# The chunked form of a bidirectional state-space scan, inside a two-block transformer kernel

## The chip, the cores and the metric

The program runs on one core of a Trainium2 chip. Its time is device microseconds for one launch, from inputs in HBM to the output in HBM; smaller is better. Before the change it takes 3826.4 us (median of three runs, 3825.4 to 3835.86).

## What is computed

The kernel computes a whole model step for 512 tokens of width 1024: a first block (a feed-forward layer, a mixer, a second feed-forward layer, with a context of 256 tokens beside it) and a second block of two layers. The change touches the mixer of the first block alone. Cut to what matters, with 12 heads in 4 groups, head width 64, state width 128:

```python
CHUNK = 128
def ssd_chunked(xs, dt, a, bm, cm, h0):          # one direction
    xdt = xs * dt[..., None]                     # per head and token
    a_cs = cumsum(dt * a)                        # inside each chunk
    seg  = exp(where(lower, a_cs[l] - a_cs[s], -inf))
    cb   = einsum('bclgn,bcsgn->bcgls', cc, bc)  # per group
    y_diag = einsum('bcgls,bcgrls,bcsgrp->bclgrp', cb, seg, xdt)
    states = einsum('bcsgn,bcgrs,bcsgrp->bcgrpn', bc, exp(a_cs[-1] - a_cs), xdt)
    h_prev = scan(h * d + s)                     # the state carried from chunk to chunk
    y_off  = einsum('bclgn,cbgrpn,bcgrl->bclgrp', cc, h_prev, exp(a_cs))
    return y_diag + y_off

y = y_forward + flip(y_backward) + d_skip * xs
y = rms_norm_per_group(y * silu(z))
out = concat([fourier_mix(u_f), y]) @ w_out
```

Both directions start from a state h0 that comes from the context.

## The kernel before

`schedule()` writes one list of steps for the whole program. Each engine walks the list and issues its own part of each step, so the list is the order of every engine's queue. `weave(F, B, rate)` merges the projections in F with a list B of other steps: a step of B is put in each time that F's matmuls have cost 1/rate us at full clock. PE, DVE, ACT and POOL each work strictly in that order, and wait on semaphores for the others.

All large products are three float32r matmuls (weights and activations each split into a high and a low part): L1244, L1245 and L1246, inside `three`. ACT makes the high part of each weight chunk (L1541), POOL the low part (L2405). PSUM has eight banks of 512 columns; six are handed out in turn (`take`, `brief`), two (6 and 7) serve the norms and the heads' sums.

The mixer, in the order of time:

- The projection to the scan's inputs ("xb"), then the same for the context ("cx"), each with convolution and transposes (L1299). Between them the step sizes `dt` and the decays `da`; step "col" (L1310) sums the decays per token.
- Step "row" (L1319) makes the cumulative decays as rows over all 512 tokens, 8 float32 matmuls of 512 columns. ACT and DVE split them into `arhl`. Step "h0" (L1339) makes the state that comes from the context.
- Then F: the projections "z" (six tiles) and "uf", and the Fourier part (L1347, L1355, L1356, L1363), whose tables come by DMA through two buffers, a load waiting for the matmul two before it. Woven into F: B, the scan, head by head.

The scan before the change treats the 512 tokens as one chunk. For a group, "grp" (L1370) makes the product of all tokens with all tokens, 4 times 128x512, which ACT copies to SBUF (L1756). For a head h, "bc" (L1379) spreads its two rows of decays over the partitions; ACT copies them out of PSUM (L1764) and takes their exponent (L1771); POOL multiplies that with `cT` (L2452) and PE applies the state to it ("hin", L1391). ACT takes the exponents of the blocks off the diagonal (step "al", L1782 and L1784) into one of two buffers `M`; for the blocks on the diagonal DVE subtracts (L2201), adds the mask (L2203), ACT takes the exponent (L1789), and DVE adds the directions (L2208), multiplies with the group's product (L2210) and adds the skip term (L2213). DVE multiplies the blocks above the diagonal (L2216), POOL those below (L2460). "u3" (L1402) sums both heads of a pair in PSUM and DVE multiplies that with z (L2223). "al" of a pair waits for "u3" of the pair before. After the heads: the groups' norm (L1797 to L2237), then the output projection.

## Time and profile before

| what | value |
|---|---|
| median of three runs | 3826.4 us |
| the profiled execution | 3825.22 us |
| its span, from the first to the last instruction | 3823.9 us |
| mean granted clock of TensorE in it | 0.963 of full |
| PE, DVE, ACT, POOL busy over the span | 93%, 45%, 39%, 39% |
| the mixer's stretch from "row" to the output projection | 810 to 1037 us |

Outside the mixer PE is busy nearly all the time. A share of busy time over the whole span says nothing of the mixer; its stretches have to be read alone, with the granted clock beside them, since at a clock of 1.2 GHz instead of 2.4 the same matmuls keep PE busy twice as long.

### The profile page before, as it was taken

The page shows a single profiled execution, that of the slowest core. Times are in us where ns is not written, and L with a number is a line of the kernel's source. Part 1 is how long each engine was busy: PE and PEld are TensorE (multiplying, and loading weights), DVE is VectorE, ACT ScalarE, POOL GpSimd, SP SyncE. Part 2 cuts the span into 40 slices and gives each one's busy share as a digit, 9 for nine tenths or more (in the row PEclk, how much of TensorE's full clock was granted, in tenths as well). Part 3 has the DMA queues.
Part 4 walks back from the last instruction along what each step waited for, and adds up shares of the span by engine and source line. Part 5 has one row for each costly group of instructions (what it writes and reads, how often), then busy time and mean ns, then how long its engine had stood idle before and what let it go on. Part 6 is the DMA issues. An engine that isn't in the chain of part 4 may idle for free.

```text
span 3823.9 us, 44699 instructions
## 1 busy us (share of the span) xinstructions
PE 3563.5 (93%) x17114; PEld 2757.9 (72%) x17114; DVE 1719.4 (45%) x3141; ACT 1496.6 (39%) x2505; POOL 1490.0 (39%) x711
## 2 busy tenths in 40 slices
PE   6999999888689998989999989999989999999998
PEld 4788889764368886866766768886867766677886
DVE  7876553546431015755552233143764553224133
ACT  3223454465442223334443334343234443334343
POOL 3554433335234444323332344444333333334443
PEclk9999999988899999989999999999999999999999
DMA  7574454221123322211112222323212222222332
GB/s 291 190 252 138 131 158 149 73 67 39 50 66 91 102 89 85 77 46 66 61 67 88 77 72 98 95 95 95 78 55 61 67 67 83 72 88 87 95 94 82
DMA packets 110981, 366.96 MB, mean 96 GB/s; under 512 B 12592, under 2 KB 13488, under 8 KB 110512
## 3 DMA queue, kind: packets, MB, share of 16 engines
q1 hardware_dynamic: 108432, 358.43, 29.0%
q10 hardware_dynamic: 2336, 5.67, 0.4%
q8 instruction: 136, 2.23, 0.2%
q14 instruction: 77, 0.63, 0.1%
HBM read 361.95 MB, written 2.10 MB: 95 GB/s over the span
## 4 chain that ended last, share of the span: by engine, by line
PE 77%; DVE 13%; ACT 5%; issue 3%; DMA 1%; POOL 1%; SPq 0%; DVEq 0%; ACTq 0%; POOLq 0%
PE ps L1244 23%; PE ps L1246 22%; PE ps L1245 22%; PE ps L1457 1%; ACT b L1541 1%; PE ps L1478 1%; DVE b L2076 1%; DVE b L2334 1%; PE ps L1439 1%; DVE b L2333 1%; DVE b L2112 1%; DVE b L2057 1%; PE ps L1402 1%; PE ps L1435 1%; DVE b L2307 1%
## 5 line engine op out<-in xcount | busy, mean ns | idle before, releaser
L2405 POOL TENSOR_TENSOR b<-b,b 128x1024 fp32r<-128x1024 f32 (+2 forms) x579 | 1324.5, 2288 | 1974.0 <-ACT b L1541 1969.1
L1244 PE MATMUL ps<-b,b 128*128 128x512 f32 (+3 forms) x4848 | 1868.0, 385 | 89.3 <-POOL b L2405 26.1
L1245 PE MATMUL ps<-b,b 128*128 128x512 f32 (+3 forms) x4848 | 1805.5, 372 | 0.0
L1246 PE MATMUL ps<-b,b 128*128 128x512 f32 (+3 forms) x4848 | 1805.3, 372 | 0.0
L1244 PEld LDWEIGHTS ps<-b,b 128*128 128x128 f32 x4848 | 935.1, 193 | 367.1 <-issue 156.7
L1246 PEld LDWEIGHTS ps<-b,b 128*128 128x128 f32 x4848 | 934.6, 193 | 162.2
L1245 PEld LDWEIGHTS ps<-b,b 128*128 128x128 f32 x4848 | 937.3, 193 | 147.1 <-issue 6.0
L1541 ACT ACTIVATE b<-b 128x1024 fp32r<-128x1024 f32 (+2 forms) x622 | 607.2, 978 | 274.3 <-PE ps L1246 242.0
L1980 DVE SCALAR_TENSOR_TENSOR b<-ps,b,b 128x511 f32<-128x511 f32 x88 | 66.0, 749 | 371.6 <-ACT b L1583 371.6
L2076 DVE CUSTOM_DVE_ANT_0 b<-b,b,b 128x1024 bf16<-128x1024 f32 x112 | 208.8, 1865 | 19.9 <-DMA b<-in_ada 8.3
L1593 ACT ACTIVATE b<-b 128x512 fp32r<-128x512 f32 (+1 forms) x110 | 64.8, 589 | 388.7 <-DVE b L1989 286.3
L2289 DVE CUSTOM_DVE_ANT_0 b<-ps,b 128x128 f32<-128x128 f32 (+2 forms) x192 | 87.5, 456 | 210.8 <-PE ps L1439 107.2
L1834 ACT ACTIVATE b<-b,b 128x128 f32<-128x128 f32 (+2 forms) x192 | 102.4, 534 | 172.3 <-DVE b L2296 130.0
L1989 DVE TENSOR_TENSOR b<-ps,b 128x512 f32<-128x512 f32 (+1 forms) x66 | 39.5, 599 | 286.9 <-PE ps L1246 286.8
L1661 ACT ACTIVATE b<-b 128x512 f32<-128x512 f32 (+1 forms) x112 | 63.9, 582 | 236.6 <-DVE b L2006 70.1
L2057 DVE TENSOR_TENSOR b<-ps,b 32x512 f32<-32x512 f32 x176 | 121.0, 687 | 68.0 <-ACT b L1627 60.7
L1848 ACT ACTIVATE b<-ps 128x128 f32<-128x128 f32 (+2 forms) x192 | 71.6, 409 | 196.0 <-PE ps L1457 194.5
L2432 POOL TENSOR_TENSOR b<-b,b 128x512 f32<-128x512 f32 x44 | 57.1, 1298 | 189.9 <-ACT b L1627 189.5
L2099 DVE TENSOR_TENSOR b<-b,b 128x512 f32<-128x512 f32 (+1 forms) x77 | 73.5, 955 | 91.7 <-ACT b L1661 91.1
L1583 ACT ACTIVATE b<-ps,b 128x512 f32<-128x512 f32 x88 | 68.5, 779 | 106.9 <-PE ps L1246 106.9
L1995 DVE TENSOR_TENSOR b<-b,b 128x512 fp32r<-128x512 f32 (+1 forms) x110 | 71.1, 646 | 80.8 <-ACT b L1593 80.8
L1457 PE MATMUL ps<-b,b 128*128 128x128 f32 x432 | 72.0, 285 | 29.2 <-DVE b L2307 28.4
(222 smaller groups left out, 2498.4 us busy)
## 6 DMA issues: line engine op xcount, KB each, us to landing
b<-in_w SPq DMA_DIRECT2D x458, 512.0 KB, 3.5
b<-in_ada SPq DMA_DIRECT2D x88, 512.0 KB, 5.4
b<-in_w SPq DMA_DIRECT2D x80, 384.0 KB, 3.1
b<-in_w SPq DMA_DIRECT2D x80, 320.0 KB, 2.9
b<-in_const SPq DMA_DIRECT2D x32, 256.0 KB, 3.5
b<-in_x SPq DMA_DIRECT2D x1, 2048.0 KB, 16.8
out<-b SPq DMA_DIRECT2D x8, 256.0 KB, 2.2
b<-in_c SPq DMA_DIRECT2D x2, 512.0 KB, 10.3
```

What stands on the lines that cost most here:

```text
L1244: pe.matmul(out, a[0], b[0], start=first, stop=False)
L1245: pe.matmul(out, a[0], b[1], start=False, stop=False)
L1246: return pe.matmul(out, a[1], b[0], start=False, stop=last)
L1457: m = pe.transpose(b[:, 128 * i:128 * i + 128], Lg[u % 6][:, 128 * i:128 * i + 128], ident)
L1541: act.activation(whi[j % NS][:, 0:nk * w], raw[j % NR][:, 0:nk * w], ACT.Copy).then_inc(up("hi", j), 1)
L1834: m = act.activation(q[:, 0:hi - lo], q[:, 0:hi - lo], ACT.Exp, bias=sx[:, 1:2], accum_out=sx[:, 2:3])
L1848: act.activation(Pt[u % 4][:, 0:hi - lo], PB[st["bank"][p]][:, 0:hi - lo], ACT.Copy).then_inc(up("pt", a, l, u), 1)
L2057: p = dve.tensor_tensor(dst[o:o + 32, i, :], b[f:f + 32, :], sin[f:f + 32, :], ALU.mult)
L2076: m = dve.tensor_tensor_reduce(spare[:, :], ada_slot(x)[:, :], cb[:, w, :], 1.0, pv("ada_b", p), ALU.mult, ALU.add, mod[:, p, w:w + 1])
L2099: dve.tensor_tensor(Q[6][:, 0:N], Q[6][:, 0:N], n_slot(nid, i)[:, 0:N], ALU.add).then_inc(up("sqa", nid, i), 1)
L2289: dve.tensor_tensor_reduce(Lg[u % 6][:, 0:w], PB[st["bank"][p]][:, 0:w], mk, 0.125, -3e38, ALU.add, ALU.max, sx[:, 0:1]).then_inc(up("t1", ...
L2405: then(pool.tensor_tensor(wlo[j % NS][:, 0:nk * w], raw[j % NR][:, 0:nk * w], whi[j % NS][:, 0:nk * w].bitcast(F32), ALU.subtract), "lop", j)
```

## The change

The scan runs in four chunks of 128 tokens, with a state per head carried between them in each direction.

- "col" sums the decays inside each chunk, and the weights of a token for its chunk's state, in one bank; "row" makes rows per chunk only, 8 matmuls of 128 columns instead of 512, and moves with "grp" into the weave of "cx". "grp" makes the four diagonal blocks of a group, and DVE multiplies them with two masks of zeros and ones as it reads them from PSUM, once per group.
- New: "bt" transposes the B projections; "ss" and "hs" make the states of the chunks (six of them, three per direction): DVE scales xs, PE makes the product, DVE scales the state before and adds.
- Per head: "bc" as before; "es" is now a minimum that DVE takes straight from PSUM (in place of ACT's copy, the subtraction and the mask); ACT takes eight exponents of 128 columns; "md" multiplies both directions with the masked product and adds the skip term. `M` has four buffers.
- Per pair: "eb" spreads the decays of the pair for the state's part and ACT takes their exponents from PSUM; "u1" sums the chunks' inner part in bank 6 or 7, "u2" the states' part in two other banks; "yv" puts them together on DVE in five instructions.
- POOL has no work of the scan left. The selection constants get a small load of their own.

```diff
-    S += weave(F, [do("sp", s="c")] + [do("gap")] * 5 + [do("ccol", i=i, d=d) for i in range(2) for d in range(2)]
-               + [do("cwg")], 0.5)
-    S += [do("row")]
+    S += weave(F, [do("sp", s="c"), do("row")] + [do("grp", g=g) for g in range(4)]
+               + [do("ccol", i=i, d=d) for i in range(2) for d in range(2)] + [do("cwg")], 0.5)
+    for g in range(4):
+        S += [do("h0", g=g, d=0), do("bt", g=g), do("h0", g=g, d=1)]
...
+    states = [do(kind, d=d, x=x) for x in range(3) for d in range(2) for kind in ("ss", "hs")]
     B = []
...
+    for k in range(7):
+        for p in range(2):
+            h = 2 * k + p
+            if h < 12:
+                B += [do("bc", h=h), do("es", h=h)] + states[:2]
+                states = states[2:]
+            if 0 < h < 13:
+                B += [do("md", h=h - 1)] + states[:2]
+                states = states[2:]
+            if k > 0:
+                B, states = B + states, []
+                B += [do("eb", k=k - 1), do("u1", k=k - 1)] if p == 0 else [do("yv", k=k - 1)]
+        if k == 5:
             B += groupnorm(0)
-    S += weave(F, B, 1.3)
+    S += weave(F, B, 1.25)
...
+            elif k == "u1":
                 x = st["k"]
                 b = bank_of(6 + x % 2)
+                at.wait_ge(*n("tc", "x", x))
+                at.wait_ge(*n("md", 2 * x + 1))
+                for i in range(4):
+                    c = slice(128 * i, 128 * i + 128)
+                    for d in range(2):
+                        for p in range(2):
+                            m = pe.matmul(b[64 * p:64 * p + 64, c], xtx[:, i, 128 * x + 64 * p:128 * x + 64 * p + 64],
+                                          M[(2 * x + p) % 4][:, d, c], start=(d == 0), stop=(d == 1))
...
+            elif k == "es":
                 h = st["h"]
                 at.wait_ge(*n("es", h))
-                act.activation(E[:, :, :], E[:, :, :], ACT.Exp).then_inc(up("ee", h), 1)
+                for d in range(2):
+                    for i in range(4):
+                        e = M[h % 4][:, d, 128 * i:128 * i + 128]
+                        p = act.activation(e, e, ACT.Exp, bias=nacol[:, i, 12 * d + h:12 * d + h + 1])
+                p.then_inc(up("ee", h), 1)
...
+                for d in range(2):
+                    at.wait_ge(*n("bc", h, d))
+                    p = dve.tensor_tensor(by_block(M[h % 4][:, d, :]), by_block(PB[st["bank"][d]][:, :]),
+                                          acol_of[:, d, :, h:h + 1].to_broadcast([128, 4, 128]), ALU.min)
+                p.then_inc(up("es", h), 1)
+            elif k == "md":
...
+                own(dve.tensor_tensor(m[:, :, :], m[:, :, :], gg[h // 3][:, :, :], ALU.mult))
+                dve.scalar_tensor_tensor(by_block(m[:, 0, :]), ident_of, pv("dskip", h), by_block(m[:, 0, :]), ALU.mult,
+                                         ALU.add).then_inc(up("md", h), 1)
+            elif k == "yv":
...
+                own(dve.tensor_tensor(a, a, PB[st["bank"][0]][:, :], ALU.mult))
+                dve.tensor_tensor(b, b, PB[st["bank"][1]][:, :], ALU.mult).then_inc(up("yo", x), 1)
+                dve.tensor_tensor(a, a, PB[6 + x % 2][:, :], ALU.add).then_inc(up("yp", x), 1)
+                at.wait_ge(*n("yp", x))
+                own(dve.tensor_tensor(a, a, b, ALU.add))
+                at.wait_ge(*n("z2", x))
+                dve.scalar_tensor_tensor(sz[:, x, :], sz[:, x, :], 0.5, a, ALU.mult, ALU.mult).then_inc(up("sz", x), 1)
```

DVE, one head of the scan before (b_125 the copied rows of decays, b_109 the column sums, b_113 the masks, b_126 the buffer E, b_134 the group's product, b_128 and b_129 the two M):

```order
L2201 TENSOR_TENSOR b_126<-b_125,b_109 128x1024
L2203 TENSOR_TENSOR b_126<-b_126,b_113 128x1024
L2208 TENSOR_TENSOR b_126<-b_126 128x512
L2210 TENSOR_TENSOR b_126<-b_126,b_134 128x512
L2213 SCALAR_TENSOR_TENSOR b_129<-b_64,b_61,b_126 128x4x128
L2216 TENSOR_TENSOR b_129<-b_129,b_134 128x384
L2216 TENSOR_TENSOR b_129<-b_129,b_134 128x256
L2216 TENSOR_TENSOR b_129<-b_129,b_134 128x128
```

DVE, one pair of heads after the change, at the place of the third and fourth projection tile (b_143 to b_146 the four M, b_133 to b_136 the groups' products, b_141 and b_142 the exponents for the states, b_81 the z tiles):

```order
L2284 TENSOR_TENSOR b_146<-ps,b_109 128x512 x2
L2293 TENSOR_TENSOR b_145<-b_145,b_133 128x1024
L2294 SCALAR_TENSOR_TENSOR b_145<-b_64,b_61,b_145 128x512
L2068 SCALAR_TENSOR_TENSOR b_81<-b_81,ps 128x512
L2301 TENSOR_TENSOR b_141<-b_141,ps 128x512
L2302 TENSOR_TENSOR b_141<-b_141,ps 128x512
L2303 TENSOR_TENSOR b_141<-b_141,ps 128x512
L2305 TENSOR_TENSOR b_141<-b_141 128x512
L2307 SCALAR_TENSOR_TENSOR b_81<-b_81,b_141 128x512
L2284 TENSOR_TENSOR b_143<-ps,b_109 128x512 x2
L2293 TENSOR_TENSOR b_146<-b_146,b_134 128x1024
L2294 SCALAR_TENSOR_TENSOR b_146<-b_64,b_61,b_146 128x512
```

A head had eight instructions; it now has four ("es" twice, "md" twice), and a pair five more that were one (L2223). The "md" of an odd head stands behind the "es" of the next even head, and "yv" of a pair stands between two heads of the next.

PE, the pair's sum before (b_59 and b_60 a pair of h, high and low; L1402 is "u3", b_128 and b_129 the two M, b_118 the transposed xs):

```order
L1246 MATMUL ps<-b_59,b_57 128x512
L1402 MATMUL ps<-b_128,b_118 64x512
L1402 MATMUL ps<-b_129,b_118 64x512
L1402 MATMUL ps<-b_128,b_118 64x512
L1402 MATMUL ps<-b_129,b_118 64x512
L1402 MATMUL ps<-b_128,b_118 64x512
L1402 MATMUL ps<-b_129,b_118 64x512
L1402 MATMUL ps<-b_128,b_118 64x512
L1402 MATMUL ps<-b_129,b_118 64x512
L1244 MATMUL ps<-b_59,b_52 128x512
```

PE after the change (L1267 to L1269 are the projections' three matmuls, L1431 "eb", b_124 `arhl`, L1443 "u1", of whose sixteen rows the first four stand here):

```order
L1269 MATMUL ps<-b_59,b_57 128x512
L1431 MATMUL ps<-b_124,b_132 128x512 x2
L1267 MATMUL ps<-b_59,b_54 128x512
L1268 MATMUL ps<-b_60,b_54 128x512
L1269 MATMUL ps<-b_59,b_57 128x512
L1443 MATMUL ps<-b_145,b_117 64x128
L1443 MATMUL ps<-b_146,b_117 64x128
L1443 MATMUL ps<-b_145,b_117 64x128
L1443 MATMUL ps<-b_146,b_117 64x128
```

Before, each pair had eight matmuls of 512 columns at "u3" and four at "hin"; now it has sixteen of 128 columns at "u1" and sixteen at "u2". "u1" and "u2" come back to back, behind the wait for the pair's second "md".

## Rows read from the trace of the kernel before

**Rows 1.** Windows: busy us of each engine by stretch, granted clock, DMA share, GB/s.
```profile
core 0: us, PE busy (x) PEld busy (x) DVE busy (x) ACT busy (x) POOL busy (x), PEclk, DMA share, GB/s
757.00:810.00 53.00, 45.99 (x327) 44.49 (x327) 20.01 (x45) 33.92 (x55) 14.30 (x6) 0.87 0.32 100
810.00:829.00 19.00, 18.48 (x61) 10.19 (x60) 6.36 (x13) 6.01 (x14) 0.00 (x0) 0.92 0.09 28
829.00:957.00 128.00, 96.88 (x380) 56.46 (x376) 81.25 (x76) 70.44 (x134) 76.49 (x54) 0.87 0.12 38
957.00:1023.00 66.00, 44.54 (x104) 13.76 (x104) 35.49 (x43) 28.72 (x53) 15.86 (x15) 0.82 0.21 56
1023.00:1037.00 14.00, 7.13 (x24) 4.28 (x24) 5.65 (x9) 7.64 (x11) 0.00 (x0) 0.93 0.00 0
```

**Rows 2.** Waits, 829 to 1023 us: who waited for whom, us, times, longest.
```profile
ACT b L1789 <- DVE b L2203: 34.9, 6, 7.5
...
DVE b L2208 <- ACT b L1789: 27.6, 12, 6.6
DVE b L2223 <- PE ps L1402: 25.3, 6, 6.2
PE ps L1402 <- DVE b L2216: 18.1, 2, 11.5
```

**Rows 3.** Groups, same stretch: DVE and ACT (count, busy us, mean ns, idle before).
```profile
L2203 DVE TENSOR_TENSOR b<-b,b 128x1024 f32<-128x1024 f32 x12 | 22.7, 1895 | 0.4
L2201 DVE TENSOR_TENSOR b<-b,b 128x1024 f32<-128x1024 f32 x12 | 15.1, 1260 | 8.8 <-ACT b L1764 8.8
L2208 DVE TENSOR_TENSOR b<-b 128x512 f32<-128x512 f32 x12 | 13.0, 1085 | 27.6 <-ACT b L1789 27.6
...
L2223 DVE SCALAR_TENSOR_TENSOR b<-b,ps 128x512 f32<-128x512 f32 x6 | 4.1, 688 | 25.3 <-PE ps L1402 25.3
...
L1782 ACT ACTIVATE b<-b,b 128x128 f32<-128x128 f32 x12 | 4.7, 391 | 0.0
...
L1771 ACT ACT_TABLE_LOAD x1 | 1.3, 1283 | 0.0
```

**Rows 4.** Timeline (start us, us, engine): DVE beside a busy POOL, and alone.
```profile
925.44 2.38 POOL L2405 TENSOR_TENSOR b<-b,b 128x1024 fp32r<-128x1024 f32 x1 [2.57 <-ACT b L1541]
...
926.27 2.10 DVE L2208 TENSOR_TENSOR b<-b 128x512 f32<-128x512 f32 x1 [1.20 <-ACT b L1789]
...
1014.02 0.69 DVE L2210 TENSOR_TENSOR b<-b,b 128x512 f32<-128x512 f32 x1
1014.75 0.75 DVE L2213 SCALAR_TENSOR_TENSOR b<-b,b,b 128x512 f32<-128x512 f32 x1
```

**Rows 5.** Timeline, PE: the pace of each shape (start, length of the run, count).
```profile
831.63 0.39 PE L1245 MATMUL ps<-b,b 128*128 128x512 f32 x1
831.86 0.39 PE L1246 MATMUL ps<-b,b 128*128 128x512 f32 x1
...
822.20 6.43 PE L1339 MATMUL ps<-b,b 128*128 128x192 f32 x32 [0.24 <-DVE b L2175]
...
863.54 3.65 PE L1402 MATMUL ps<-b,b 128*64 128x512 f32 x16
...
1684.95 1.09 PE L1478 MATMUL ps<-b,b 128*64 128x128 f32 x16
...
1764.31 1.03 PE L1457 MATMUL ps<-b,b 128*128 128x128 f32 x8
```

**Rows 6.** The same, PE, behind a wait: the same shape at the lower clock.
```profile
1016.66 5.93 PE L1402 MATMUL ps<-b,b 128*64 128x512 f32 x16 [11.52 <-DVE b L2216]
```

**Rows 7.** Chain of work that ended last (start us, us, what).
```profile
810.14 8.40 PE ps L1319 x16
```

**Rows 8.** Instructions of line L1347 (min/median/max ns, first and last start), and its waits.
```profile
L1347 PE MATMUL ps<-b,b x32: 592/592/1050, 957.4 to 994.0; 128*128 128x512 f32 x32
...
  DMA b<-in_const: 15.5, 13
```

More of the change, by code:

```diff
@@ L355, in schedule @@
             F.late.append(do("turn", s="x", m=m - 4))
-    S += weave(F, addnorm(1) + squares(5) + prenorm(3) + [do("sp", s="x")] + [do("gap")] * 6
-               + [do("col", i=i) for i in range(4)], 0.5)
+    S += weave(F, addnorm(1) + squares(5) + prenorm(3) + [do("sp", s="x")] + [do("gap")] * 6 + [do("col")], 0.5)
     F = fore()
@@ L722, in number @@
         elif k == "col":
-            s["bank"] = [brief(), brief()]
-            for d in range(2):
-                mark("col", s["i"], d)
-                mark("colv", s["i"], d)
+            s["bank"] = brief()
+            mark("col")
+            mark("wte")
+            mark("wxv")
+            mark("colv")
         elif k == "row":
@@ L1406, in pe_program @@
+                    for i in range(4):
+                        c = slice(128 * i, 128 * i + 128)
+                        for p in range(2):
+                            h = 2 * x + p
+                            m = pe.matmul(b[64 * p:64 * p + 64, c], state(d, i if d == 0 else 3 - i)[:, 64 * h:64 * h + 64],
+                                          cT[:, h // 3, c], start=True, stop=True)
+                    freed[st["bank"][d]] = ("yo", x)
+                m.then_inc(up("u2", x), 1)
             elif k == "gn2":
@@ L1727, in act_program @@
                 at.wait_ge(*n("h0p", g, d))
[L1728 removed]
+                act.activation(h0[:, d, 192 * g:192 * g + 192], PB[st["bank"]][:, 0:192], ACT.Copy).then_inc(up("h0", g, d), 1)
             elif k == "row":
[L1730 removed]
                 at.wait_ge(*n("row"))
@@ L2156, in dve_program @@
             elif k == "col":
[L2157 removed]
                 at.wait_ge(*n("lna"))
[L2159 to L2164 removed]
+                at.wait_ge(*n("wte"))
```

421 lines of the change are left out of this document (215 added, 206 removed), and 6 rows, old and new, of the table SIGNALS.

## The prediction

> **What bounds the kernel now.** I read the windows first. From 829 to 1037 us, where the scan is woven into the projections, no engine is full: in the first 128 us PE is busy 97, DVE 81, ACT 70, POOL 76, at a granted clock of 0.87 [rows 1]. So what ends the stretch is a loop between engines. The waits name it: ACT's diagonal exponent (L1789) waits for DVE's mask (L2203) 34.9 us in six waits, DVE's next step (L2208) waits for that exponent 27.6 us in twelve, DVE's pair step waits for PE's sum 25.3 us, and PE's sum waits for DVE's last product (L2216) up to 11.5 us at once [rows 2]. "al" of a pair also waits for the sum of the pair before, so pairs hardly overlap. Ahead of it stands the row step alone on PE, 8.4 us [rows 7]; behind it the groups' norm, 14 us [rows 1].
>
> The Fourier part has another limit. Its 16 matmuls run from 957.4 to about 995 us, waiting 15.5 us for tables [rows 8]: two buffers, each load released by the matmul two before. That stays.
>
> **Prices.** DVE: 512 columns from SBUF 0.69 us, the skip term 0.75 [rows 4], 512 with a PSUM operand 0.69 (L2223), 1024 columns 1.26 (L2201) [rows 3]. Between 512 and 1024, 768 columns are about 0.97; 384 from PSUM about 0.55, below the 0.69. PE, at the pace of a run: a projection matmul 0.23; 64 weight columns by 128 moving, the shape of "u1" and "u2", 16 rows in 1.09, so about 0.055 a row; 128 by 128 eight in 1.03, 0.13 a row; 128 by 192 32 in 6.43, 0.20 a row [rows 5]. A float32 matmul is two rows. ACT: 128 columns 0.39 at most, a table load 1.28 [rows 3].
>
> **The change, stretch by stretch.** The span of 3823.9 us is walked in the windows of [rows 1].
>
> *Up to 810 us.* "row" (16 rows) and four "grp" (32 rows) enter the weave of "cx": 48 x 0.13 = 6.2 us, where PE is busy 46 of 53 us, so mostly exposed; taken as +5. The masks (four 1024-column products, 5 us of DVE) hide there, since DVE has 33 us free; uncovered they would cost those 5. "col" goes from 40 rows to 34, nothing. Its new exponent on ACT brings a table load and one back, 2.6 us, in a stretch bound by PE: +0.5, between 0 and 2.6. The constants' own load stands before DVE's first work: between 0 and 0.5, taken at 0.5 at most and inside the +0.5. Sum **+6**, between 0 and 10.
>
> *810 to 829.* The 8.4 us of "row" go, and "grp" of group 0 and the split of the rows, which stood beside DVE's scaling. Left are the 32 rows of "h0", 6.4, and 16 transposes at 0.13, 2.1, plus the first scaling: 10 of 19 us. **-9**, between -10 and -6.
>
> *829 to 957, with the projections z and uf.* After the change the weave puts four pairs' "u1" and "u2" here, as many as before. PE would need 144 x 0.23 + 96 x 0.12 = 45 for the projections, 10 for "ss" (48 x 0.20), 6 for "bc" and "eb", 16 for four pairs at 64 x 0.055 = 3.5 plus 0.4 of first latency: 77 us. DVE decides, in two phases. Until the first pair: three "es" (6 x 0.69 = 4.1), two "md" (2 x (1.26 + 0.75) = 4.0), six states (each 0.97 + 0.97 + 2 x 0.55 = 3.0, together 18), z 1.4: 27.5, plus 2 before the first "bc", plus the slowing below, about 4, plus the pair on PE, 4: **38**. Then a cycle per pair. DVE's queue has two "es" 2.8, two "md" 4.0, "yv" 5 x 0.69 = 3.5, and 1.5 z tiles 1.0: 11.3. It cannot run through, since "bc" of the next head stands behind "u1" and "u2" in PE's queue: DVE idles while PE does both (3.9), three projection matmuls (0.7) and "bc" (0.4), 5.0; and "bc" of the head after takes a bank that "yv" has to free, 0.6 more. Together 16.9, plus 1.3 for POOL: 18.2. PE's own work in a cycle is 12 to 13, so PE waits some 5 us in each. Three cycles are 55, then 2 us until the Fourier part: 38 + 55 + 2 = 95 of 128. **-33**. Between PE's 77 (-51) and no more than a third of it (-11).
>
> The slowing: POOL's low part of a weight chunk stays, 1.3 a cycle. L2208 took 2.10 beside it and the same shape 0.69 alone [rows 4], 1.4 us more; instructions with a PSUM operand (L2223) stay at 0.69 in the mean [rows 3]. I take 1.0 per chunk since half of DVE's instructions read PSUM. The Trainium skill ("SBUF — State Buffer", section "Who interferes with whom") says that a DVE instruction with two SBUF inputs is held for the whole of a GpSimd instruction that reads SBUF. By that rule a chunk could cost up to 2.4 us, and four and a half cycles some 8 us more than my sum.
>
> A rule against the change: the Trainium skill ("VectorE: DVE Perf Modes", section "The TRN2 errata") gives DVE a larger fixed cost for a PSUM source, 120 cycles against 58. L2223 reads PSUM and takes 0.69, as L2210 from SBUF does [rows 3, 4], so the sum has no such cost. By the page the 55 or so reads from PSUM would add about 4 us.
>
> *957 to 1023.* 38 us of Fourier matmuls at the tables' pace, then its last two products with their copies, 6, then the last pair, 4: 48 of 66. Before, the last pair's "al" to "u3" still stood behind all that (L1402 starts at 1016.66 [rows 6]). In the new list the last "md" is ahead of the norm of the first half, with two pairs' DVE work of 22 us inside 38: hidden; uncovered it would cost up to 15. **-18**, between -22 and -5.
>
> *1023 to 1037.* The last "yv" is five instructions where one was: 4 x 0.69 = **+3**.
>
> The lower clock: behind a wait the same 16 rows took 5.93 us in place of 3.65 [rows 5, 6]. PE will wait in each cycle, and "u1" and "u2" of 3.9 us stand on the path: at half clock 3.9 more. I take it for one pair in three to one in six: **+4**, between 0 and 16.
>
> POOL loses all its scan work; it was no term of the path except through DVE.
>
> Sum: 6 - 9 - 33 - 18 + 3 + 4 = **-47 us**. The profiled execution took 3825.2 us, 1.3 more than its span, and comes to 3778; it lies 1.2 below the median of 3826.4, so the forecast of the median is **3779 us**.
>
> **Rivals.**
> - *PE becomes the bound* (0.12). DVE's cycle is shorter than its queue, because "es" and "md" slip beside "u1" and "u2". For it: PE's 77 us are 18 less than the 95. Against it: the order of "bc" behind "u2". With the clock's cost gone too: 6 - 9 - 51 - 21 + 3 = -72, 3754 us.
> - *The gain is given back in part* (0.12). The handshakes of the cycle are dearer (ACT's queue holds the pair's exponent and the weights' split ahead of a head's eight exponents, 3.1 us), and the clock is low for most pairs: 5 us a cycle over five cycles, 25 us. -22, 3804 us.
> - *Slower than before* (0.02): PE at the lower level, 1.2 of 2.4 GHz, through the whole woven stretch. PE's work there is 77 plus about 30 in the Fourier part and the last pair; at half the clock it is 214 against the 194 us that the two stretches take. With the other terms, 20 + 6 - 9 + 3 = +20, 3846 us. It decides from a granted clock under about 0.6 over the stretch; it was 0.87 and 0.82 with longer waits than I expect [rows 1]. The Trainium skill ("TensorE: Matmul & The Clock Gate", section "HAM oscillation") warns that short bursts between waits keep TensorE slow; the five-us waits of my cycle are such.
> - *No change* (0.04): DVE is the bound in another place, for instance the states of the six chunks come one after the other through PE, 18 us of DVE doubled by waits, and the cycle stays at 26 us, as far apart as pairs are now (128 us for four of them and part of a fifth): about 3822 us.
>
> **How the numbers follow.** The forecast with its own range, 3762 to 3795, has 0.70. The range that holds 8 of 10 goes out to the first rival and most of the second: 3752 to 3806. A measurement of this kernel tells about 0.3%, 11.5 us. Faster by more than that: 0.70 + 0.12 + 0.12 and nothing of the rest, rounded down to 0.93 for a stall that I don't see; within it 0.04, slower 0.03.
>
> **What the new profile would show.** Right: no scan work on POOL; first projection of z near 825 us, Fourier matmuls from about 920; pairs of "u1" some 18 us apart while DVE is busy about 12 of them; 16 rows of "u1" in about 1.1 us; the Fourier part still near 38 us. Wrong: "u1" closer than 15 us (first rival); rows of "u1" at twice the length, a granted clock near 0.7 (second); the first "u1" much later than 38 us into z (the states); a Fourier part with DVE steps of heads behind it; a stretch up to 810 us that is longer by more than 10.

## The result and the profile after

The changed kernel takes 3806.7 us (median of five runs, 3798.8 to 3811.9) against 3826.4: 0.9941 of the time before, interval 0.9923 to 0.9960. The two medians alone would give 0.995. A second set of five runs gave 3807.3 us and the same 0.9941 (0.9928 to 0.9955). So the change saves 20 us, where 47 were forecast: the direction was right, the size was not. The time lies outside the forecast's own range (3762 to 3795) and just outside the wider one (3752 to 3806). It is where the second rival stood (3804, the gain given back in part).

The profiled execution took 3808.7 us with a span of 3807.4. Its windows have the columns of [rows 1], with 957 to 1023 cut in two:

```profile
core 0: us, PE busy (x) PEld busy (x) DVE busy (x) ACT busy (x) POOL busy (x), PEclk, DMA share, GB/s
829.00:957.00 128.00, 98.83 (x620) 77.47 (x620) 74.39 (x94) 45.40 (x121) 18.27 (x8) 0.85 0.18 52
...
957.00:995.00 38.00, 23.79 (x88) 9.84 (x84) 16.26 (x22) 16.84 (x32) 0.00 (x0) 0.96 0.18 49
995.00:1023.00 28.00, 17.94 (x83) 12.43 (x80) 9.74 (x14) 8.46 (x11) 2.40 (x1) 0.70 0.00 1
1023.00:1037.00 14.00, 14.00 (x64) 11.58 (x63) 1.38 (x2) 6.54 (x9) 5.43 (x3) 1.00 0.34 112
```

Over 829 to 957, ACT went from 70 to 45 us and POOL from 76 to 18, but DVE only from 81 to 74, and PE is hardly busier than before, though the work comes sooner: the output projections, which began at 1037, run at the full clock by 1023. No engine is full here either. The waits from the first z projection to the output projections say between whom the time goes (who waits, for whom, us, times, longest):

```profile
DVE b L2284 <- PE ps L1423: 38.8, 8, 10.5
ACT b L1819 <- DVE b L2284: 33.4, 10, 5.7
...
PE ps L1412 <- DVE b L2227: 11.0, 5, 4.6
...
PE ps L1423 <- DVE b L2302: 6.6, 2, 3.5
...
PE ps L1431 <- ACT b L1676: 5.0, 1, 5.0
DVE b L2243 <- PE ps L1412: 4.9, 4, 2.2
```

L1423 is "bc", the row sums of a head on PE; L2284 is DVE's step "es" on them; L1819 the head's exponents; L1412 is "ss", a chunk's state on PE, L2227 its input "sx" and L2243 its sum on DVE. The long waits of [rows 2] (exponent on mask, product on exponent, PE's sum on DVE's product) are gone, and a wait of DVE for PE's row sums has come in their place. In the first stretch, up to 872 us, PE and DVE wait for each other in turn. In the next three cycles PE waits 12.4 us, and 11.6 of them are for banks: twice for "yv" of the pair before (L2302, 6.6 us), once for ACT's copy of uf (L1676, 5.0 us).

What the groups cost, DVE, the same stretch (count, busy us, mean ns, idle before), to be read beside [rows 3]:

```profile
L2293 DVE TENSOR_TENSOR b<-b,b 128x1024 f32<-128x1024 f32 x12 | 16.1, 1341 | 0.0
L2284 DVE TENSOR_TENSOR b<-ps,b 128x512 f32<-128x512 f32 x24 | 15.5, 684 | 38.8 <-PE ps L1423 38.8
...
L2227 DVE TENSOR_TENSOR b<-b,b 128x768 f32<-128x768 f32 x6 | 7.9, 1323 | 0.0
L2237 DVE TENSOR_TENSOR b<-b,b 128x768 f32<-128x768 f32 x6 | 7.8, 1307 | 0.0
...
L2243 DVE TENSOR_TENSOR b<-b,ps 128x384 f32<-128x384 f32 x12 | 6.1, 550 | 5.1 <-PE ps L1412 4.9
```

PE's timeline, the first pair and the last (start us, length of the run, engine, line, shape, count, idle before):

```profile
872.17 1.97 PE L1443 MATMUL ps<-b,b 128*64 128x128 f32 x32
873.96 1.92 PE L1455 MATMUL ps<-b,b 128*64 128x128 f32 x32
...
994.00 2.46 PE L1443 MATMUL ps<-b,b 128*64 128x128 f32 x32 [2.86 <-DVE b L2294]
996.24 3.14 PE L1455 MATMUL ps<-b,b 128*64 128x128 f32 x32
1003.67 2.07 PE L1464 MATMUL ps<-b,b 128*128 128x512 f32 x2 [4.29 <-ACT b L1845]
1005.54 1.92 PE L1465 MATMUL ps<-b,b 128*128 128x512 f32 x2
```

The first pair takes 3.7 us for 64 rows of "u1" (L1443) and "u2" (L1455), the last 5.4; L1464 and L1465 are the sums of the groups' norm. The five pairs before the last all take 3.7 to 3.8.

Set against the forecast, stretch by stretch, from landmarks in the two timelines:

| stretch | landmarks before | after | forecast | measured |
|---|---|---|---|---|
| to the end of the context's projections | 809.6 | 814.8 | +6 | +5.3 |
| to the first z projection | 829.2 | 825.8 | -9 | -8.7 |
| z and uf, to the first Fourier matmul | 957.4 | 939.6 | -33 | -14.4 |
| Fourier part and last pair, to the end of its last product | 1022.6 | 999.4 | -18 | -5.4 |
| to the output projections behind the norm | 1037.0 | 1019.2 | +3 | +5.4 |
| lower clock | | | +4 | inside the others |
| rest of the span | | | 0 | +1.3 |
| sum | | | -47 | -16.5 |

Two terms carry the miss, 19 us in z and uf and 13 in the Fourier part. Inside z and uf: from the first z projection to the end of the first pair's "u2" 50.1 us where 38 were forecast; then the next three "u2" end 18.8, 18.2 and 21.2 us apart where 18.2 each was forecast; then 5.6 us to the Fourier part, not 2.

The landmarks move as a whole by what comes ahead of the mixer: the first matmul of "cx" starts at 766.8 before and 767.8 after. So 1.0 of the +5.3 lies ahead of this stretch, and from that matmul to the first z projection it is 62.5 us before and 58.0 after.

### The profile page after: what moved, and what is told of

Its sections match the earlier page's. It is cut to its first block, busy times and chain, and to the rows that moved or that the text cites. A ratio compares the mean times of both kernels' runs of the same rounds, so it can differ in the third digit from the quotient of the medians.

```text
span 3807.4 us, 45164 instructions
## 1 busy us (share of the span) xinstructions
PE 3554.7 (93%) x17424; PEld 2788.7 (73%) x17424; DVE 1701.4 (45%) x3133; ACT 1465.6 (38%) x2478; POOL 1418.5 (37%) x651
## 4 chain that ended last, share of the span: by engine, by line
PE 77%; DVE 13%; ACT 5%; issue 2%; DMA 2%; POOL 1%; SPq 0%; DVEq 0%; POOLq 0%; ACTq 0%
PE ps L1267 23%; PE ps L1269 22%; PE ps L1268 22%; PE ps L1510 1%; ACT b L1594 1%; PE ps L1531 1%; DVE b L2124 1%; DVE b L2417 1%; PE ps L1492 1%; DVE b L2416 1%; DVE b L2160 1%; DVE b L2105 1%; POOL b L2488 1%; PE ps L1488 1%; DVE b L2390 1%
## 5 line engine op out<-in xcount | busy, mean ns | idle before, releaser
L1267 PE MATMUL ps<-b,b 128*128 128x512 f32 (+3 forms) x4848 | 1866.6, 385 | 88.7 <-POOL b L2488 26.1
L1269 PE MATMUL ps<-b,b 128*128 128x512 f32 (+3 forms) x4848 | 1806.4, 373 | 0.0
L1267 PEld LDWEIGHTS ps<-b,b 128*128 128x128 f32 x4848 | 936.4, 193 | 357.6 <-issue 147.8
L1269 PEld LDWEIGHTS ps<-b,b 128*128 128x128 f32 x4848 | 936.2, 193 | 161.3
```

Source lines behind the costliest of these rows:

```text
L1267: pe.matmul(out, a[0], b[0], start=first, stop=False)
L1269: return pe.matmul(out, a[1], b[0], start=False, stop=last)
```

## The experiments

All are changes to the changed kernel, and "sooner" is against its own trace. Positions are given from the first z projection on, since its start moves between 817 and 827 us from run to run and from kernel to kernel. One set of runs tells some 0.15% (6 us) in the whole time. Each set had its own runs of the kernel before, so two kernels of different sets are compared by their ratios to it as well as by their medians.

How much one trace tells can be seen from the last run below, the changed kernel unchanged, traced a second time. From z's start to the output projections behind the norm it takes 193.9 us, against 193.4 in the first trace. Inside, the two differ by one to two microseconds: the first "u1" at 45.0 and 46.4 us, the Fourier matmuls 47.6 and 46.5, the last pair's 64 rows 3.7 and 5.4.

### The state's input one chunk ahead

```diff
+    S += [do("sx", d=d, x=0) for d in range(2)]
     S += weave(F, B, 1.25)
...
@@ DVE
-            elif k == "ss":
-                d, x = st["d"], st["x"]
+            elif k == "sx" or k == "ss" and 0 < 2 * st["x"] + st["d"] < 5:
+                d, x = (st["d"], st["x"]) if k == "sx" else (1 - st["d"], st["x"] + st["d"])
```

> The changed kernel, with one edit: DVE makes the product that a chunk's state matmuls read (sx) one chunk ahead, in place of right before those matmuls. Same instructions, other order on DVE only. In the changed kernel the first u1 starts 46 us after the first projection of z (826.0 to 872.2), and PE waits 11 to 12 us for sx in five waits. Theory A (turn-taking: PE and DVE wait for each other because each hands over its step only just before the other needs it): PE's waits for sx fall below 3 us, the first u1 comes 8 to 12 us sooner (34 to 38 us after z's start), the program takes 3795 to 3800. Rival B (DVE's own time decides: its instructions are slowed beside POOL, 2.4 to 3.1 us in place of 0.95, and PE's wait only shows that): the waits move from sx to hs or bc, the first u1 comes at most 3 us sooner, 3803 to 3807.

Measured: 3796.4 us (0.9918 of the kernel before, 0.9904 to 0.9933). The first "u1" starts 35.4 us behind z's start, not 46.4. The waits of PE in that stretch, where the changed kernel had the 11.0 us shown above (L1416 is here "ss", L1427 "bc", L2247 the sum of a state):

```profile
PE ps L1416 <- DVE b L2247: 2.2, 1, 2.2
PE ps L1427 <- DVE b L2247: 0.9, 1, 0.9
PE ps L1416 <- DVE b L2231: 0.6, 1, 0.6
```

PE's waits for "sx" (L2227, here L2231) fell from 11.0 us to 0.6, the stretch became 11.0 us shorter, and the program 10.3 (9 by the ratios). Theory A holds: the two engines took turns, and the place of one DVE instruction was nearly the whole loss. Not all of the 11.0 us are the edit's, though. The granted clock of 826 to 860 is 0.83 in the changed kernel's first trace and 0.95 here, but it is 0.95 in its second trace too, where the first "u1" starts at 45.0; against that trace the edit brings 9.6.

### Another bank for the second half of the Fourier part

```diff
             if s["i"] == 0:
+                turn[0] += 2 if (s["m"], s["cs"]) == (1, 0) else 0
                 fo_bank = take()
```

> The changed kernel, with one edit: the second half of the Fourier matmuls takes a PSUM bank two turns further on, one that no product of a head pair holds. In the changed kernel its first matmul waits until 968.2 for the bank that yv of pair 4 frees (8.8 us of such waits), and the Fourier matmuls take 46.5 us against 38 before the change. Theory A (the bank's wait is the loss): the part takes 38 to 41 us, the program 3799 to 3802. Rival B (the tables' transfers, 15.5 us of waits before, pace it anyway and the bank's wait only lies over theirs): the wait turns into one for a table, the part takes 44 us or more, 3804 to 3807.

Measured: 3806.2 us (0.9948, 0.9934 to 0.9963), no difference that these runs can tell; the Fourier matmuls took 42.9 us, not 46.5. PE's timeline at the place, the changed kernel and then this one:

```profile
963.16 1.10 PE L1387 MATMUL ps<-b,b 128*128 128x512 f32 x2 [0.78 <-ACT b L1803]
968.22 3.56 PE L1371 MATMUL ps<-b,b 128*128 128x512 f32 x4 [3.96 <-DVE b L2302]
```
```profile
964.08 1.88 PE L1372 MATMUL ps<-b,b 128*128 128x512 f32 x4
967.92 1.97 PE L1372 MATMUL ps<-b,b 128*128 128x512 f32 x2 [1.96 <-DMA b<-in_const]
```

The matmul no longer waits 4.0 us for "yv" of pair 4 (L2302), which stands in DVE's queue behind the Fourier result's subtraction; it starts 4.1 us sooner, and the next but one then waits 2.0 us for a table. At the end of the part 3.6 us are left, between the two theories; of the 8.5 us that the part took beyond the forecast this is 3.6. The program's time is where rival B has it. The trace of this kernel is 6 us shorter from z's start to the output projections behind the norm (187.1, not 193.4), and the medians and ratios do not show that; this stays open.

### Row sums ahead of the pair

```diff
-                B += [do("bc", h=h), do("es", h=h)] + states[:2]
+                B += ([do("bc", h=h)] if k == 0 or p == 0 else []) + [do("es", h=h)] + states[:2]
@@
             if k > 0:
                 B, states = B + states, []
+                B += [do("bc", h=h + 1)] if p == 0 and k < 6 else []
                 B += [do("eb", k=k - 1), do("u1", k=k - 1)] if p == 0 else [do("yv", k=k - 1)]
```

> The changed kernel, with one edit: the row sums (bc) of a pair's second head stand on PE ahead of the pair step before (eb, u1, u2), not behind it, so that DVE can work while PE does that step. This also shifts the turn of the banks, so the Fourier matmuls' wait for the bank of pair 4 goes. Theory A (a cycle is a chain of hand-offs, PE's step then DVE's): the ends of u2 of pairs 0 to 3 come 13 to 15 us apart, not 18 to 21; with the bank's wait gone, 12 to 20 us less in all, 3787 to 3795. Rival B (the cycle is bound by PE, whose own work is 12 to 13 us at the full clock and longer at the lower): 17 to 18 us apart, and only the bank's 6 us are gained, 3799 to 3804.

Measured: 3786.2 us (0.9897, 0.9881 to 0.9914), 20 us less than the changed kernel. Windows from the end of the first "u2" to that of the fourth, the changed kernel and then this one:

```profile
875.90:934.00 58.10, 45.75 (x352) 38.98 (x352) 34.83 (x42) 24.75 (x66) 9.52 (x4) 0.88 0.15 46
```
```profile
877.20:925.30 48.10, 41.58 (x357) 36.15 (x355) 35.91 (x42) 24.75 (x67) 9.53 (x4) 0.96 0.17 56
```

Three cycles take 48.1 us, 16.0 each, not 58.1, with DVE and ACT doing the same work; PE is busy 4.2 us less for as many instructions, at a granted clock of 0.96 and not 0.88. The Fourier matmuls took 38.4 us, as before the change; PE's waits in them are for tables now (9.7 us in seven). The cycles came out between the two theories, one microsecond over A's upper end; the whole is just below A's lower one.

The edit does two things at once, beside the clock, and these runs do not part them. It moves the row sums ahead, and it shifts the turn of all banks behind. DVE's wait for the row sums in these windows falls from 10.8 us to 0.5. But PE's two waits for the bank of "yv" (6.6 us) and the one for ACT's copy of uf (5.0 us, in the third cycle) are gone too, and in their place stand waits of 2.6 us for DVE's z step and 1.4 for ACT's copy of uf. The third cycle gained most: 14.7 us, not 21.2, where the first two took 15.9 and 17.4, not 18.8 and 18.2.

### Both orders together, and the clock

Both edits, the state's input ahead and the row sums ahead, nothing else:

> The changed kernel with the two orders together: DVE's product for a state made one chunk ahead, and the row sums of a pair's second head ahead of the pair step on PE. Alone they took the first u1 from 46.4 to 35.4 us behind z's start (10 us of the program), and the cycles of the pairs from 58.1 to 48.1 us with the Fourier matmuls from 46.5 to 38.4 (20 us of the program). Theory A (separate stalls in a row, so they add): 3806.7 - 10.3 - 20.4 = 3776, between 3773 and 3780. Rival B (the second order already hides part of the first's wait, or the weights' stream, which the scan then overtakes, becomes the bound): 3781 to 3786.

Measured: 3781.2 us (0.9886, 0.9870 to 0.9903). The first "u1" is 36.5 us behind z's start and the Fourier part takes 39.9 us, within some 1.5 us of the two kernels alone, but from the last Fourier matmul to the end of the last pair it is 17.1 us where the row sums ahead alone had 11.6. That is rival B's time without rival B's place; the 5 us between it and theory A are less than one set of runs tells. The timeline shows little more than half the pace in each of these instructions (L1384 is a product of the Fourier part's end):

```profile
952.29 2.07 PE L1384 MATMUL ps<-b,b 128*128 128x512 f32 x2 [0.69 <-ACT b L1804]
...
962.23 3.68 PE L1448 MATMUL ps<-b,b 128*64 128x128 f32 x32 [2.48 <-DVE b L2299]
965.70 2.96 PE L1460 MATMUL ps<-b,b 128*64 128x128 f32 x32
```

6.4 us for the 64 rows that take 3.7, in a stretch (940 to 985) with a granted clock of 0.70. Two kernels test the clock by itself, with matmuls whose result is overwritten, in waits of PE. On the changed kernel:

```diff
                 b = bank_of(6 + x % 2)
+                for i in range(8 if x == 5 else 0):
+                    pe.matmul(b[:, :], pick[:, 0, :], arhl[:, :], start=True, stop=True)
                 at.wait_ge(*n("tc", "x", x))
@@ norm
+                if hf == 1:
+                    b = bank_of(st["bank"][0])
+                    for i in range(14):
+                        pe.matmul(b[:, :], pick[:, 0, :], arhl[:, :], start=True, stop=True)
                 at.wait_ge(*n("gs", hf, 2))
```

> The changed kernel; PE gets matmuls whose result is overwritten, in two of its waits: 8 before the last pair's u1 (it waits 2.9 us there) and 14 before the second sums of the groups' norm (4.3 us). It measures what the lower clock costs in the tail. In the changed kernel the last pair's 64 rows took 5.4 us at the lower clock against 3.7 for the first pair's, and the eight rows of the norm's sums 6.3 against some 3.7 before the change. Theory A (the clock falls because PE stands idle there): 64 rows in 3.7 to 3.9, the norm's sums in 2.2 to 3.8 us, the first output projections at 0.23 and not 0.43 apart; together 3 to 5 us less, 3801 to 3804. Rival B (the clock does not come back within such a stretch, and the added work only delays the waited-for step): rows as long as before, 0 to 3 us more, 3806 to 3810.

Measured: 3801.9 us (0.9940, 0.9925 to 0.9955). The median is 5 us below the changed kernel's, but the ratio is the same (0.9941 in both its sets): the program's time does not show a gain.

```profile
990.10 2.03 PE L1438 MATMUL ps<-b,b 128*128 128x512 f32 x8
993.12 1.97 PE L1445 MATMUL ps<-b,b 128*64 128x128 f32 x32 [1.00 <-DVE b L2300]
994.92 1.92 PE L1457 MATMUL ps<-b,b 128*64 128x128 f32 x32
996.77 3.54 PE L1466 MATMUL ps<-b,b 128*128 128x512 f32 x14
1001.13 1.12 PE L1470 MATMUL ps<-b,b 128*128 128x512 f32 x2 [0.82 <-ACT b L1851]
1002.10 1.02 PE L1471 MATMUL ps<-b,b 128*128 128x512 f32 x2
...
1014.01 0.80 PE L1267 MATMUL ps<-b,b 128*128 128x512 f32 x1 [5.73 <-DVE b L2326]
1014.60 0.63 PE L1268 MATMUL ps<-b,b 128*128 128x512 f32 x1
```

The pair's 64 rows take 3.7 us and the norm's sums 3.1 to the start of the next matmul (5.8 in the changed kernel). The second trace of the changed kernel, without any added matmul, is the fairer one to set beside it:

```profile
994.53 1.97 PE L1443 MATMUL ps<-b,b 128*64 128x128 f32 x32 [2.48 <-DVE b L2294]
996.33 1.92 PE L1455 MATMUL ps<-b,b 128*64 128x128 f32 x32
1002.54 1.84 PE L1464 MATMUL ps<-b,b 128*128 128x512 f32 x2 [4.29 <-ACT b L1845]
1004.17 1.92 PE L1465 MATMUL ps<-b,b 128*128 128x512 f32 x2
```

There the 64 rows take 3.7 us as well, behind a wait of 2.5 us; so the eight matmuls before the pair are not shown to have done anything. The norm's sums take 4.8 there, as in every other trace whose last pair ran at the full clock and whose wait was 4.3 us. The fourteen matmuls before them kept a clock that was still full (they took 3.5 us themselves), and from the end of the last pair to the first output projection it is 7.4 us and not 9.1. That 1.7 us is what the filling is shown to bring. Behind the next wait, 5.7 us with nothing to fill it, the first projections still stand 0.43 apart: that part of theory A failed, and shows the same thing from the other side. The Trainium skill ("TensorE: Matmul & The Clock Gate", section "HAM oscillation") says that short bursts between waits keep TensorE slow; these rows agree.

The same matmuls, word for word, on the kernel with both orders:

> e4_both with the overwritten matmuls of e6_keep_busy (8 before the last pair's u1, 14 before the second sums of the norm). e4_both missed the sum of its two parts by 5 us; in its trace the last pair's 64 rows took 6.4 us (3.7 in e3_bc_ahead) and the norm's sums 6.2. Theory A (the parts add, but the earlier end of the scan left PE at the lower clock in the tail, 0.70 over 940 to 985): rows and sums come back to 3.7 to 3.9 and 3.1 to 3.8 us, 4 to 7 us less than e4_both, 3774 to 3777. Rival B (the loss is elsewhere, in waits that the second order had hidden already): at most 3 us less, 3778 to 3782.

Measured: 3773.4 us (0.9855, 0.9839 to 0.9871), the lowest median here and 8 us less than without them (by the two ratios 0.3%, with intervals that just meet). From the last Fourier matmul to the end of the last pair it is 11.6 us again. PE's timeline, the product of the Fourier part's end and the last pair:

```profile
946.53 1.13 PE L1384 MATMUL ps<-b,b 128*128 128x512 f32 x2 [0.69 <-ACT b L1810]
...
953.72 1.97 PE L1450 MATMUL ps<-b,b 128*64 128x128 f32 x32 [1.00 <-DVE b L2305]
```

From z's start to the first output projection this trace is 9.8 us shorter than that of the kernel with both orders. Of these, 4.5 us lie ahead of the last pair's "u1", and they cannot come from the added matmuls: those stand behind the Fourier part, whose end already ran at the full clock here (L1384 in 1.13 us) and at the lower one there (2.07). The pair's rows are another 2.7, which differ by 1.7 between two traces of the changed kernel too, and 2.5 come from the end of the pair on. So in the traces the two orders add, and what hid it was the lower clock behind them; but only the norm's part of that is shown to be cured by the added matmuls. Why the clock fell at the end of the Fourier part in one trace and not in the other was not tested.

### POOL's work on the weights left out

```diff
-                then(pool.tensor_tensor(wlo[j % NS][:, 0:nk * w], raw[j % NR][:, 0:nk * w],
-                                        whi[j % NS][:, 0:nk * w].bitcast(F32), ALU.subtract), "lop", j)
+                v = 16 if STREAM[j][0] in ("z", "uf") else nk * w
+                then(pool.tensor_tensor(wlo[j % NS][:, 0:v], raw[j % NR][:, 0:v],
+                                        whi[j % NS][:, 0:v].bitcast(F32), ALU.subtract), "lop", j)
```

> The changed kernel, but POOL forms the low part of 16 columns only of each weight chunk of z and uf (the other columns keep old values, so this part of the computation is left out). POOL's seven long instructions (2.4 to 2.8 us each) beside the scan shrink to about 0.1. Theory A (hand-offs): DVE's instructions with two SBUF inputs go back to 0.7 to 1.3 us, some 6 to 8 us less from z's start to the end of the fourth pair's u2, most of it where DVE is waited for; 3799 to 3802. Rival B (POOL's slowing explains most of the 12 us that the stretch to the first pair took beyond the forecast): first u1 at 36 us or sooner, 3794 to 3797. Rival C (slowed instructions are slack, since PE's steps decide): at most 2 us, 3804 to 3807.

Measured: 3797.9 us (0.9924, 0.9909 to 0.9939). From z's start to the end of the fourth "u2" it takes 101.1 us, not 108.3 (107.5 in the second trace); the first "u1" comes only 2.8 us sooner (1.4 against the second trace). DVE's groups of 768 columns (L2237 and L2227):

```profile
L2237 DVE TENSOR_TENSOR b<-b,b 128x768 f32<-128x768 f32 x6 | 5.7, 954 | 0.0
L2227 DVE TENSOR_TENSOR b<-b,b 128x768 f32<-128x768 f32 x6 | 5.7, 950 | 0.0
```

They fall from 1.31 and 1.32 us in the mean to 0.95, close to the 0.97 of the forecast. Theory A holds; rival B, POOL as the cause of the late first pair, gets at most 3 of its 12 us. POOL costs 6 to 7 us over this stretch, where the forecast had 4 up to the first pair and 1.3 for each cycle, 8 in all: that term was right in its sum.

### The Fourier tables left out

```diff
+                if x >= 2:
+                    continue
                 a = CAT[("cl", "sl")[x // 4 % 2]] + 512 * (x % 4)
@@ PE
-                at.wait_ge(s[f"d_tab{x % 2}"], 16 * (x // 2 + 1))
+                at.wait_ge(s[f"d_tab{x % 2}"], 16)
```

> The kernel with the row sums ahead (e3_bc_ahead), but only the first two of the 16 Fourier tables are loaded and all 16 steps use these two (so the Fourier part is wrong: 14 loads of 256 KB and the waits for them are left out). There the Fourier matmuls took 38.4 us, the same 38 us as before the change. Theory A (the transfers pace them, each load released by the matmul two before): without them 15 to 25 us for the part, and the program 10 us or more below 3786, at 3768 to 3776, if nothing else ends later. Rival B (the head steps and the norm's chain beside it end as late, so the part is short but the last pair waits for DVE and ACT): the part under 28 us, the program only 0 to 8 us below, 3778 to 3786.

Measured: 3777.3 us (0.9872, 0.9854 to 0.9891), 9 us less than with the tables (14 of the 16 loads are left out); the part takes 27.4 us, not 38.4. So 11 us of the part are the tables' pace. In the trace 7 of them reach the output projections: the last pair now waits 4.3 us for DVE, not 2.9, and its rows run at the lower clock (5.4 us).

```profile
960.83 3.60 PE L1446 MATMUL ps<-b,b 128*64 128x128 f32 x32 [4.27 <-DVE b L2297]
```

That is rival B's picture; the time lies between the two theories. Of the 27 us that are left, some 14 are these 32 rows themselves (ten of them take 4.45 us), the rest pair steps, copies and sums that stand between them. The claim that the 38 us stay was right as a floor; the changed kernel did not reach it.

### A faster weave

Both orders, and:

```diff
-    S += weave(F, B, 1.25)
+    S += weave(F, B, 1.35)
```

> e4_both with the scan's steps woven in faster (1.35 steps per us of fore work, not 1.25), which puts the last pair and the first half's norm ahead of the last Fourier steps, not behind them. Theory A (the last pair stands alone behind the Fourier part, 10 us from the last product to the end of its u2, only because of its place in the list): another 6 to 10 us less than e4_both, 3766 to 3770. Rival B (the steps now come before their inputs are ready and PE waits for DVE with projections queued behind): within 3 us of e4_both, or slower.

Measured: 3775.4 us (0.9870, 0.9855 to 0.9885), 6 us less than both orders at the old rate, which is at the edge of what the runs tell (0.9886). The last pair now runs at the full clock between Fourier matmuls (1.97 and 1.92 us) and ends its "u2" 142.1 us behind z's start, not 147.3. But the first "u1" comes 41.5 us behind, not 36.5, and the Fourier part takes 44.6: both theories have a share. That the steps now come closer together than DVE can feed them is likely, but no run tests it. With the loop of overwritten matmuls before the norm's sums, here `range(8)`, and none before the pair:

> e8_rate135 with 8 overwritten matmuls before the second sums of the norm, where PE waits 2.2 us. There the last pair already runs at the full clock inside the Fourier part, and the sums took 5.3 us. Theory A (what is left of the tail's clock is worth its rows): sums in 3.1 to 3.5 us, 2 us less than e8_rate135, 3772 to 3775. Rival B (added matmuls outlast the wait at the lower clock): 3775 to 3779.

Measured: 3775.6 us (0.9862, 0.9849 to 0.9876). The sums took 3.1 us, not 4.8; a difference of that size is below what these runs can tell, and A and B meet at this time. It stays open in the whole time.

### The row step and the groups' products alone again

```diff
-    S += weave(F, [do("sp", s="c"), do("row")] + [do("grp", g=g) for g in range(4)]
-               + [do("ccol", i=i, d=d) for i in range(2) for d in range(2)] + [do("cwg")], 0.5)
+    S += weave(F, [do("sp", s="c")] + [do("gap")] * 5 + [do("ccol", i=i, d=d) for i in range(2) for d in range(2)]
+               + [do("cwg")], 0.5)
+    S += [do("row")] + [do("grp", g=g) for g in range(4)]
```

> The changed kernel with one part of the change undone: row and the four grp stand behind the context's projections again, alone on PE (16 and 32 rows, with ACT's copy and DVE's two subtractions and four mask products of 1.26 us), not woven into them. Theory A (as forecast: PE paces the context's projections, so what stands in them costs its 6.2 us there as it does behind them; only DVE's masks, 5 us, and the hand-offs of row lose their cover): 0 to 5 us more than the changed kernel, 3807 to 3812. Rival B (the weave hid the rows in PE's waits, so they come on top when they are taken out): 6 to 11 us more, 3813 to 3818. Rival C (the masks hide behind h0 here as well, and the shorter row costs no more than in the weave): 3804 to 3807.

Measured: 3811.4 us (0.9962, 0.9948 to 0.9975), 4 to 5 us more than the changed kernel by the medians and 8 by the ratios. PE's timeline:

```profile
807.85 3.39 PE L1344 MATMUL ps<-b,b 128*128 128x128 f32 x16
811.02 3.97 PE L1396 MATMUL ps<-b,b 128*128 128x128 f32 x32
818.56 1.62 PE L1364 MATMUL ps<-b,b 128*128 128x192 f32 x4 [3.56 <-DVE b L2260]
```

The rows take 7.1 us alone, and behind them PE waits 3.6 us for DVE, which masks and scales (1.2 us in the changed kernel). The projections of "cx" take 39.7 us from their first matmul to their last, as before the change, and 44.0 in the changed kernel: woven in, the rows cost 4.2 there. From the first "cx" matmul to the first z projection it is 62.2 us, against 58.0 and 57.7 in the two traces of the changed kernel. So undoing this part costs 4.2 to 4.5 us where the edit stands. That is theory A's amount, and below the 6 of rival B, which the whole time alone would not exclude.

The changed kernel was also run again, as it is, beside the two kernels that have both orders or the faster weave together with added matmuls:

> The changed kernel once more, on the chip and in the rounds of the two kernels beside it, so that they can be set against it and not only against the kernel before. Any theory: 0.992 to 0.996 of the kernel before, 3803 to 3811 us; first u1 some 46 us behind z's start, Fourier matmuls about 46.5 us.

Measured: 3807.3 us (0.9941, 0.9928 to 0.9955), first "u1" 45.0 us behind z's start, Fourier matmuls 47.6 us. The waits that the account below rests on are there again: PE's 6.6 and 5.0 us for banks in the three cycles, and 4.0 for the bank in the Fourier part. PE waits somewhat longer for "sx", 12.6 us in six waits. What is not there again is the lower clock in the last pair.

## Why the prediction was right and wrong

**Right: prices.** The rows of "u1" and "u2", 0.055 to 0.06 us each (64 in 3.7), DVE's 0.69 for 512 columns with or without a PSUM operand (L2284: 684 ns), 0.75, 0.55 and the 0.95 of 768 columns alone, the masks hidden in the context's stretch. The terms up to z came to within a microsecond by the landmarks, within two when the drift ahead of the mixer is taken off, and undoing that part lengthened the stretch by 4.2 to 4.5 us, within theory A. The Trainium skill's higher fixed cost of a PSUM source ("VectorE: DVE Perf Modes", section "The TRN2 errata") is again not in the rows: L2284 reads PSUM 24 times at 684 ns.

**Wrong: "Until the first pair ... 38".** This term missed by 12 us. It was a sum of DVE's instructions with one allowance of 2 us before the first row sum, as if DVE ran through. The order of the two queues says otherwise: "sx" stands right before the scaling of the state and behind "es" and "md" of the head before, and PE's "ss" stands in front of the projections. PE waits for "sx" (11.0 us in five waits), DVE then waits for "ss" (4.9 us in four). Making "sx" one chunk ahead took 11.0 of the 12 us away, 9.6 of them against the second trace; POOL's share was at most 2.8 in its own experiment. The prediction did name such a thing, in the "no change" rival ("the states of the six chunks come one after the other through PE"), but gave it no price in the sum.

**Nearly right: "a cycle per pair", 18.2.** Measured 18.8, 18.2 and 21.2. That two of them fit so well is in part luck, since terms were missed both ways. The reason given, "bc" of the next head behind "u1" and "u2", is what the third experiment removed, and with the shift of the banks it brought 3.3 us a cycle of the 5.0 that were put on it. The wait for the bank that "yv" frees was put at 0.6 a cycle; it measured 6.6 us in two waits. The third cycle also holds PE's wait of 5.0 us for ACT's copy of uf (L1676), which frees the bank of "eb", and the later start of the Fourier part (5.6 us, not 2) a wait of 3.0 us for the last such copy: the sum had neither.

**Wrong: "38 us of Fourier matmuls at the tables' pace".** It was taken over from before the change as if only the tables could end there. Measured 46.5 (47.6 in the second trace). The new banks put the second half's first matmul behind "yv" of pair 4, and that behind a subtraction that waits for ACT: 3.6 us by the second experiment. The other 4.9 went with the bank and the order of the row sums together; the runs do not tell which step of the pair holds them. With both gone the part is at 38.4, and the tables' pace is its floor.

**Misplaced: the lower clock.** "+4, between 0 and 16". In the first trace it is paid where PE waits before a run of its own: 1.7 us in the last pair, 2.7 in the norm's sums. In the second trace the last pair does not pay it, and the norm's sums pay 1.7. Through the cycles the granted clock was 0.88 with the waits and 0.96 with most of them gone. That PE would wait in each cycle was right; the place was not: I put it on the pairs between the projections, and the five pairs ahead of the last ran at the full clock (3.7 to 3.8 us for 64 rows, one 4.4 in the second trace), while the tail had it. The tail's +5.4 in place of +3 is this: with the waits filled the same stretch took 17.2 us, 2.8 more than before the change. The size of the term, +4 in all, was not measured by itself.

**The sum.** 12 (states), 3 (third cycle), 3.6 (start of the Fourier part), 8.5 (its matmuls), 3.3 (last copies and last pair, 13.3 us and not 10), 2.4 (tail) and 1.3 (rest) are 34; less the 4 that stood aside for the clock, which is within them, this is the 30 between -47 and -16.5. The two orders and the filled waits together bring the program to 3773, below the 3779 of the forecast: the gain was there, and most of it was given back at hand-offs between PE and DVE, at banks, and in the clock behind them.

## What to carry to other kernels

When work moves from a full engine to a chain over two, the durations of its instructions are not its price: read both queues in order, and write down for each step which instruction of the other engine stands in front of it. A producer wants to stand one step ahead of its consumer's queue, and a step that only feeds another engine belongs ahead of a long one, not behind it; here two such moves, without one instruction less, took the program from 0.994 to 0.989 of the time before, nearly as much as the change itself had done. A new PSUM bank order brings new waits with it (11.6 us in three cycles and 4.0 in the Fourier part here), and moving a step shifts the banks of all steps behind it, so one edit can test two causes. A wait on TensorE can be paid again behind it, at half the clock; whether it is differs between two traces of the same kernel, so a claim on it wants the unchanged kernel traced twice.

## What the runs showed of the hardware

- A few matmuls without use keep the clock. With fourteen of them (3.5 us) in a wait that was there anyway, the norm's eight rows took 3.1 us behind them; without them they took 4.8 in the second trace of the changed kernel and 5.8 in the first. The clock was full when they began, so they kept it and did not bring it back. Eight of them (2.0 us) before the last pair are not shown to help: its 64 rows took 3.7 us behind them, but 5.4 and 3.7 in two traces without them.
- The same kernel meets the lower clock in other places from trace to trace. The changed kernel's granted clock over 826 to 860 us was 0.83 in one trace and 0.95 in the other, with both profiled executions within 1 us of each other in time.
- DVE beside POOL. The same 768 columns took 0.95 us in one place and 3.10 in another; the second began at 840.84, beside a POOL instruction of 2.70 us that began at 840.42. With POOL's instruction cut to 16 columns all twelve such instructions took 0.95. DVE's "es" and "yv" instructions that read PSUM keep their 0.67 to 0.69 either way. The Trainium skill ("SBUF — State Buffer", section "Who interferes with whom") has it so: only the port pair that the two share is fought over.

```profile
840.84 3.10 DVE L2237 TENSOR_TENSOR b<-b,b 128x768 f32<-128x768 f32 x1
```
```profile
840.42 2.70 POOL L2488 TENSOR_TENSOR b<-b,b 128x1024 fp32r<-128x1024 f32 x1 [10.48 <-ACT b L1594]
```
